# A two-layer transformer chain on one core: the recurrence's output projection, the order inside the head projections, the forget rows and the exponential's table

## The reference

```
out = (yn + bonus) * g ;  y = out @ w_out
x = layernorm(4**0.25 * x + (1 + gt1) * y)
```

```
q_a = rope(rmsnorm(q)) ; k_b = rmsnorm(kf) ; q_b = rmsnorm(qf)
logits_b = q_b k_b / 8 + cum(log f)[query] - cum(log f)[key]
```

## Time and profile before

| | |
|---|---|
| median of 3 runs | 2915.62 us (2913.86 to 2916.25) |
| the profiled execution | 2917.28 us |
| its span | 2915.5 us |
| PE busy | 2770.7 us, 95% |
| DVE, ACT, POOL busy | 1360.3, 1012.8, 300.4 us |
| mean granted clock of TensorE | 0.97 |

### The profile page before, as it was taken

The page is one execution under the profiler, slowest core; times in us unless marked ns, Lnnn a source line. Parts: engine busy times, 40 slices in busy tenths (PEclk is TensorE's granted clock), DMA queues, the critical chain, the costliest instruction groups (busy, mean ns, idle before and its releaser), DMA issues.

```text
span 2915.5 us, 46457 instructions
## 1 busy us (share of the span) xinstructions
PE 2770.7 (95%) x19096; PEld 2018.3 (69%) x19096; DVE 1360.3 (47%) x2285; ACT 1012.8 (35%) x1570; POOL 300.4 (10%) x250
## 2 busy tenths in 40 slices
PE   7999998899999899989999899999989899999999
PEld 4566666478888535678888778887565567788886
DVE  6566565243333266653333544333224776434335
ACT  5334333143422124644432333221111465323223
POOL 3232332010000003210000010000000131000000
PEclk9999999999999999999999999999979999999999
DMA  5333433222232121022232122322021001222331
GB/s 221 114 124 129 139 123 123 102 87 92 95 108 95 48 66 37 26 91 101 88 115 100 58 81 91 106 99 100 31 75 70 1 9 66 101 92 95 114 110 58
DMA packets 46292, 261.07 MB, mean 90 GB/s; under 512 B 5128, under 2 KB 7576, under 8 KB 26168
## 3 DMA queue, kind: packets, MB, share of 16 engines
q1 hardware_dynamic: 45128, 254.23, 24.8%
q10 hardware_dynamic: 1008, 4.57, 0.4%
HBM read 256.63 MB, written 2.15 MB: 89 GB/s over the span
## 4 chain that ended last, share of the span: by engine, by line
PE 87%; DVE 5%; ACT 3%; issue 1%; POOL 1%; PEld 1%; DMA 1%; SPq 0%; DVEq 0%; ACTq 0%; PEldq 0%; POOLq 0%
PE psum L214 86%; PE psum L2064 2%; PEld psum L214 1%; DMA ada_first<-in_ada_first 1%; POOL branch_in L564 0%; POOL ysum L562 0%; DVE residual L1539 0%; ACT L608 0%; POOL join L557 0%; DVE weights L248 0%; DVE residual L1531 0%; DVE keys_rstd L2675 0%; DVE cmp_blocks L2689 0%; ACT ln_in L1494 0%; ACT nsa_probs L2100 0%
## 5 line engine op out<-in xcount | busy, mean ns | idle before, releaser
L214 PE MATMUL psum<-ffn_in_hi,ffn_weights_hi 128*128 128x512 f32 x768 | 305.0, 397 | 12.4 <-DVE ffn_weights_lo L1660 7.8
L1657 ACT ACTIVATE ffn_weights_hi<-weights 128x1024 fp32r<-128x1024 f32 (+1 forms) x128 | 145.9, 1142 | 490.7 <-PE psum L214 490.7
L214 PE MATMUL psum<-ffn_in_lo,ffn_weights_hi 128*128 128x512 f32 x768 | 302.0, 393 | 0.0
L214 PE MATMUL psum<-ffn_in_hi,ffn_weights_lo 128*128 128x512 f32 x768 | 301.9, 393 | 0.0
L214 PE MATMUL psum<-ff_in_hi,ff_weights_hi 128*128 128x512 f32 x704 | 277.6, 394 | 11.5 <-DVE ff_in_lo L1545 7.2
L1657 ACT ACTIVATE ff_weights_hi<-weights 128x1024 fp32r<-128x1024 f32 (+1 forms) x120 | 137.6, 1147 | 433.4 <-PE psum L214 433.4
L214 PE MATMUL psum<-ff_in_lo,ff_weights_hi 128*128 128x512 f32 x704 | 276.7, 393 | 0.0
L214 PE MATMUL psum<-ff_in_hi,ff_weights_lo 128*128 128x512 f32 x704 | 276.3, 392 | 0.0
L1660 DVE TENSOR_TENSOR ff_weights_lo<-weights,ff_weights_hi 128x1024 fp32r<-128x1024 f32 (+1 forms) x116 | 156.3, 1347 | 253.4 <-ACT ff_weights_hi L1657 253.4
L1660 DVE TENSOR_TENSOR ffn_weights_lo<-weights,ffn_weights_hi 128x1024 fp32r<-128x1024 f32 (+1 forms) x126 | 166.9, 1327 | 110.4 <-ACT ffn_weights_hi L1657 110.3
L214 PEld LDWEIGHTS psum<-ffn_in_hi,ffn_weights_hi 128*128 128x128 f32 x768 | 146.2, 190 | 47.2 <-DVE ffn_weights_lo L1660 9.1
(11 more groups left out here) (519 smaller groups left out, 4899.3 us busy)
## 6 DMA issues: line engine op xcount, KB each, us to landing
weights<-in_ff_in SPq DMA_DIRECT2D x44, 1024.0 KB, 4.7
weights<-in_ffn_in SPq DMA_DIRECT2D x44, 1024.0 KB, 4.7
weights<-in_ada SPq DMA_DIRECT2D x80, 512.0 KB, 3.5
weights<-in_ff_out SPq DMA_DIRECT2D x16, 1408.0 KB, 5.9
weights<-in_ffn_out SPq DMA_DIRECT2D x16, 1408.0 KB, 5.9
weights<-in_rwkv SPq DMA_DIRECT2D x8, 1152.0 KB, 5.6
weights<-in_fox_qkv SPq DMA_DIRECT2D x4, 1536.0 KB, 6.4
weights<-in_rwkv SPq DMA_DIRECT2D x8, 640.0 KB, 4.0
```

The lines of the kernel that those rows point to most:

```text
L214: return nc.tensor.matmul(out, lhsT, rhs, start=start, stop=stop)
L1657: return nc.scalar.activation(sp_.hi[u][:, 0:width], slot[s][:, u * width:(u + 1) * width], ACT.Copy)
```

## The change

Four edits. The recurrence's output projection goes from `project` to `split_project`; the recurrence's output is split tile by tile on ACT (`recurred_hi`) and DVE (`recurred_lo`), PE waits for each tile of it by itself (`by_tile`), and the residual is loaded in four quarters which POOL multiplies, DVE waiting for a quarter at the head of each output tile (`x_by_tile`). In `head_inputs` the key's sum stands behind the first block of the value products and the rotation behind the second; ACT's root of the key stands ahead of its copy of the values. The clearing of the forget rows is appended to POOL's list before the head projections. And each `paired_attention` begins on ACT with an exponential of one column into an array that nobody reads.

```diff
         def residual_again(ready):
-            act_done = steps("again_act", ["scaled"])
+            done = steps("again_pool", [f"scaled{q}" for q in range(4)])
+            quarter = x_in
 
             def act(act):
-                act_done.enter(act)
                 for r in ready:
                     act.wait_ge(*reached(*r))
-                act.dma_start(x[:, :, :], d["x"][:, :, :]).then_inc(x_in[0], 16)
-                act.wait_ge(x_in[0], 32)
-                nc.scalar.activation(x[:, :, :], x[:, :, :], ACT.Copy, scale=ALPHA).then_inc(*act_done.step("scaled"))
-
-            phase(act=act)
-            return act_done, "scaled"
+                for q in range(4):
+                    act.dma_start(x[:, 2 * q:2 * q + 2, :], d["x"][:, 2 * q:2 * q + 2, :]).then_inc(quarter[q], 16)
+
+            def pool(pool):
+                done.enter(pool)
+                for q in range(4):
+                    pool.wait_ge(quarter[q], 32)
+                    nc.gpsimd.tensor_scalar(x[:, 2 * q:2 * q + 2, :], x[:, 2 * q:2 * q + 2, :], ALPHA, None, ALU.mult, ALU.bypass).then_inc(
+                        *done.step(f"scaled{q}"))
+
+            phase(act=act, pool=pool)
+            return lambda j: (done, f"scaled{j // 2}")
...
-        def split_project(halves, stream, source, ready, factor, x_ready, units_free=None, into=None, gain=None, later=None, following=None, roots=None):
+        def split_project(halves, stream, source, ready, factor, x_ready, units_free=None, into=None, gain=None, later=None, following=None, roots=None, x_by_tile=None, by_tile=False):
...
-                        if j == 0 and not roots:
+                        if j == 0 and not roots and not by_tile:
                             for r in ready[u]:
                                 pe.wait_ge(*reached(*r))
                         for k in range(half):
                             if roots:
                                 roots.between(pe, j, u, k)
-                                if j == 0:
-                                    pe.wait_ge(*reached(*ready[u][k]))
+                            if (roots or by_tile) and j == 0:
+                                pe.wait_ge(*reached(*ready[u][k]))
...
                 for j in range(KT):
                     i, s = j // 2, j % 2
+                    if x_by_tile:
+                        dve.wait_ge(*reached(*x_by_tile(j)))
...
         STEP_TILES = (2, 3, 1, 0)
 
+        unread = keep("table_unread", [P, 1])
...
             def act(act):
+                nc.scalar.activation(unread[:, :], const("rms_eps"), ACT.Exp)
                 if made is not None:
                     made.act(act, 0, TR)
...
-            pe_done = steps("heads_pe", ["nq", "fq", "nq sum", "fk", "fq sum", "v", "rot", "fk sum"])
-            act_done = steps("heads_act", ["nq sq", "fq sq", "nq std", "fk sq", "fq std", "v", "fk std"])
+            pe_done = steps("heads_pe", ["nq", "fq", "nq sum", "fk", "fq sum", "fk sum", "rot", "v"])
+            act_done = steps("heads_act", ["nq sq", "fq sq", "nq std", "fk sq", "fq std", "fk std", "v"])
...
                     for b in range(QT):
                         for k in range(KT):
                             last = mm(ps[:, V, b * P:(b + 1) * P], h[:, k, b * P:(b + 1) * P], wtile(1, 2 * KT + k), k == 0, k == KT - 1)
+                        if b == 0:
+                            pe.wait_ge(*act_done("fk sq", i))
+                            mm(ps[:, KSUM, :], blockones, sq["fk"][:, :]).then_inc(*pe_done.step("fk sum"))
+                        if b == 1:
+                            pe.wait_ge(*dve_done("nq n", i))
+                            mm(ps[:, ROT, :], cc("rot"), qn[:, :]).then_inc(*pe_done.step("rot"))
                     last.then_inc(*pe_done.step("v"))
-                    pe.wait_ge(*dve_done("nq n", i))
-                    mm(ps[:, ROT, :], cc("rot"), qn[:, :]).then_inc(*pe_done.step("rot"))
-                    pe.wait_ge(*act_done("fk sq", i))
-                    mm(ps[:, KSUM, :], blockones, sq["fk"][:, :]).then_inc(*pe_done.step("fk sum"))
...
+                    root("fk", KSUM, "fk", i)
                     act.wait_ge(*pe_done("v", i))
                     alone(act)
                     nc.scalar.activation(tile_of(out["fox_v"], i), ps[:, V, :], ACT.Copy).then_inc(*act_done.step("v"))
-                    root("fk", KSUM, "fk", i)
...
-            return out, [(dve_done, "fk", N - 1), (act_done, "fk std", N - 1)]
+            return out, [(dve_done, "fk", N - 1), (act_done, "v", N - 1)]
...
             scaled = residual_again([recurred])
-            summed = project("rwkv_out", "rwkv_out", [yout[:, k, :] for k in range(KT)], [recurred], (0, GT1), [scaled])
+
+            def recurred_hi(act, name=name, turn=turn):
+                hi_done.enter(act)
+                act.wait_ge(*reached(rec_done, name, turn - 1))
+                out_units.first(act, out_units.first_hi)
+                for k in range(KT):
+                    act.wait_ge(*reached(rec_done, name, k))
+                    nc.scalar.activation(recurred_parts[0][:, k, :], yout[:, k, :], ACT.Copy).then_inc(*hi_done.step(f"hi{k}"))
+
+            def recurred_lo(dve):
+                lo_done.enter(dve)
+                out_units.first(dve, out_units.first_lo)
+                for k in range(KT):
+                    dve.wait_ge(*hi_done(f"hi{k}"))
+                    nc.vector.tensor_tensor(recurred_parts[1][:, k, :], yout[:, k, :], recurred_parts[0][:, k, :].bitcast(F32), ALU.subtract).then_inc(
+                        *lo_done.step(f"lo{k}"))
+
+            phase(act=recurred_hi, dve=recurred_lo)
+            summed = split_project(out_units, "rwkv_out", [(recurred_parts[0][:, k, :], recurred_parts[1][:, k, :]) for k in range(KT)],
+                                   [[(lo_done, f"lo{4 * u + k}") for k in range(4)] for u in range(2)], (0, GT1), (), x_by_tile=scaled,
+                                   by_tile=True)
...
-                    heads, ready = head_inputs(parts, h, cc, ready)
+                    nsa_q = keep("heads_nsa_q", [P, 4, T], parts)
                     sides, zero_sides = forget_sides(parts, ready)
+                    phase(pool=zero_sides)
+                    heads, ready = head_inputs(parts, h, cc, ready, nsa_q)
                     with ExitStack() as own:
                         nsa_done = grouped_attention(own, heads["nsa_q"], t, cc, ready, mixed[:, 0:4, :])
-                    phase(pool=zero_sides)
```

8 lines of the change are left out of this document (6 added, 2 removed).

## The result

| | before | after |
|---|---|---|
| median of the runs (4 each) | 2915.93 us | 2898.59 us (2897.08 to 2899.59) |
| the profiled execution | 2917.28 us | 2898.09 us |
| mean granted clock | 0.97 | 0.972 |

The ratio is 0.9928, 95% interval 0.9915 to 0.9941; the same two kernels, measured twice more, gave 0.9941 (0.9927 to 0.9954) and 0.9931 (0.9918 to 0.9944). Their mean, 0.9933, is 19.4 us of 2915.62. The ratio is not the quotient of the two medians beside each other: these differ by 17.3 us here and by 15.0 and 19.3 us in the two others. The forecast was 13.6 us, 2902.0 us, with a range from 2898.0 to 2909.0. The median of 2898.59 lies just inside the range, but the ratio of 0.9928 puts the kernel at 2894.6 us and the mean of the three at 2896.2, faster than the whole range.

What follows compares the result with a forecast made beforehand. TensorE was taken to bound the kernel, holding 87% of the chain of waits. Terms 6.2 + 2.7 + 0.8 + 2.7 + 1.2 = 13.6 us gave a median of 2902.0 us, range 2898.0 to 2909.0.

Steps and rivals of the forecast that it cites:

- for clock gained elsewhere: Whole kernel: the range was said to go 3 us beyond the high end for this.
- Projection, term 6.2 us: Recurrence's output projection: split one-pass products shorten the stage from 57.6 to 51.4 us, gaining 6.2 us (2.5 to 7.3).
- the sign that the scaled quarters end before 541: Recurrence's output projection: if the forecast is right, POOL's scaled residual quarters end before 541 us.
- Order, term 2.7: End of the head projections: key sum and rotation inside the value products bring everything after 2.7 us earlier (2.4 at least).
- nothing is gained in the first turns: Head projections: in the three other turns PE never waited, so the new order gains nothing there.
- Table, term 0.8: Grouped attention's start: table load leaves the place between mask and first exponential, gaining 0.8 us (0 to 1.3).
- Rows, terms 2.7 + 1.2: Grouped attention's start: without memsets the scaling pair falls 2.7 us (or 0); clock behind it gives 1.2 (0 to 2.0).
- the stall of another cause: Attention's first scaling pair: memsets didn't make the stall, so 2.7 and 1.2 us are missing, 2905.9 us; chance 0.10.
- the clock stuck low: Recurrence's output projection: PE's clock stays low, slower, up to 2939.1 us if for all 192 products; chance 0.03.
- the late residual: Recurrence's output projection: DVE waits for the first quarter, gain 2.5 instead of 6.2 us, 2905.7 us; chance 0.12.

Runs made afterwards that it cites:

- residual_only: Kernel before with only the residual loaded in four quarters and multiplied on POOL, projection still float32; 2917.05 us, ratio 0.9992.
- sp_loads: Changed kernel with the four residual loads on SyncE's queue, behind the first two rows of weights, instead of ACT's; 2900.37 us, ratio 0.9932.
- best: sp_loads plus unread PE products in holes ahead of this projection and the head projections, and a finer order of splits; 2902.46 us, ratio 0.9936.
- proj_only: Kernel before with only the recurrence's output projection changed to the new split one; 2908.94 us, ratio 0.9962.
- loads_later: Changed kernel with the four residual loads on ACT's queue behind its source splits instead of ahead of them; 2906.02 us, ratio 0.9956.
- before_again: Kernel before, unchanged, measured again as a kernel of its own; 2919.45 us, ratio 0.9998.
- after_again: Changed kernel, unchanged, measured a second time; 2904.98 us, ratio 0.9941.
- best2: best with DVE's wait for the scaled quarter moved from ahead of the weights' split to the update of x; 2898.61 us, ratio 0.9934.
- rows_only: Kernel before with only the clearing of the forget rows moved ahead of the head projections; 2913.67 us, ratio 0.9977.
- rows_twice: Changed kernel with the six memsets made a second time at their old place behind the head projections; 2905.37 us, ratio 0.9949.
- wait_at_update: sp_loads with DVE's wait for the scaled quarter moved from ahead of the weights' split to the update of x; 2899.61 us, ratio 0.9933.

## Why the prediction was right in its mechanisms and wrong in its sum

The mechanisms held; the sum was too small. The step that failed is the clock's share in it: I counted low stretches only inside the stages whose work I changed, and put every other stage at nothing.

- What was put at 0: F and X, 1.5 us each. No work in them changed, yet the low stretch at their start is gone in all three profiles of the changed kernel. This is the largest part of what was missing.
- The margin for it was too small as well. The prediction says that the range goes 3 us beyond the high end "for clock gained elsewhere", but its end at 2898.0 lies 1.6 us beyond the 2899.6 of the high ends. With 3 us it would have been 2896.6, still a little above the mean of the three measurements, 2896.2.
- Projection, term 6.2 us. In the two profiled executions it is 57.67 to 51.5, 6.15 us, with the start at 4.69 (forecast 4.5), some nine low products (forecast 10.3) and no wait for the residual. But the profiled execution of before was one of the short ones. From POOL's end to the end of the projection the mean of six profiles with the old projection is 58.1 us and that of the five of the changed code 51.4, so the term is 6.7 us. P as a whole, 85.3 and 78.1, is 7.1 us shorter: the other 0.4 lie in the first feed-forward's first products.
- The residual: the sign that the scaled quarters end before 541 failed. They ended at 542.8, 15.9 us behind POOL's last tile where 541 meant 12.6, and it cost nothing here. A quarter took POOL 2.77 us even with DVE idle (residual_only), not 2.2.
- The conflict of POOL and DVE. The low parts of the weights took DVE 1.38 and 1.51 us in the changed kernel where they began with a multiply of POOL, and 0.69 us otherwise; in sp_loads one took 0.68 us that began 2.2 us into POOL's second multiply. The Trainium skill (GPSIMD Engine Reference, 1. Specifications) says that GpSimd shares its SBUF interfaces with VectorE and contends with instructions that have two SBUF inputs, as these have: the slow ones agree, the one in the middle of a multiply shows no contention. It cost nothing in the changed kernel. In best some 2.0 of the 2.77 us of PE's hole are this slowing (an estimate: 3.95 us for POOL's first quarter against 2.77, and 1.52 for the split against 0.69); the rest is the place of the wait.
- Order, term 2.7: 2.5 alone. In the three profiles of the changed kernel H is 3.6 us shorter; most of the other 1.1 lies at its first 16 products, which took 15.2 to 15.6 us instead of 16.4. proj_only, which has the old order, is 0.7 us shorter there too, and loads_later, which has all four edits, is not (16.3). I had said that nothing is gained in the first turns.
- Table, term 0.8: 0.9, and up to 1.8 while the memsets are still there. Rows, terms 2.7 + 1.2: 2.7 and 1.7, the latter with the doubt above. Together A fell from 96.3 to 91.0, 5.3 us against 4.7. The two overlap: alone they gave 2.1 and 4.4.

By the table the changed stages sum to 7.1 + 3.6 + 5.3 + 1.5 + 1.5 = 19.0 us, against 19.4 by the mean of the ratios. That they agree so well is in part luck, for the stages outside the table move by several us from profile to profile: the profiles of before and after differ by 19.2 us in all, those of before_again and after_again by 13.7.

Open is why the low stretches in F, in the first products of H and in X come and go. In F, 5 of 6 profiles with the same code as before up to there have it and none of the eight with the new projection and a cold start, but residual_only lacks it too, and best and best2 have it. F's length goes with how late the clock rose a few microseconds earlier; which edit, if any, decides that was only argued. The rivals: the stall of another cause is refuted by rows_only and rows_twice; the clock stuck low did not occur; the late residual is real but had 0.2 us or less of effect until PE ran its first tile at the full clock.

## What to carry to other kernels

A hole in TensorE's stream can be paid for twice, once as idle time and once as a low clock behind it. Stages that nobody touched can lose or gain such a low stretch: widen the range on the gaining side by one (1.5 us here) for each later stage that begins with one in the profile before, and on the other side for each that could get one. When a single stage gets shorter and the kernel doesn't, look for these stretches first, and profile the unchanged kernel more than once before you call a difference of this size an effect. Put a wait right ahead of the instruction that needs it: a wait for the residual ahead of the next weights' split cost nothing until the stage got faster, and then was part of a hole of 2.8 us. And read which event an engine's first instruction really waited for, since a wait ahead of it in the queue can hide an earlier start of 1.6 us.

## What the runs showed of the hardware

- A memset of 1 x 2048 or 128 x 2048 on POOL takes 1.8 to 1.9 us. Beside memsets a pair of DVE scalings of 128 x 384 with two column operands ended 0.2 us behind the end of one: 0.87 us alone, 2.65 to 3.58 beside them. A scaling of 128 x 8 took 1.86 us through one memset and 3.60 through two (before_again), against 0.23 alone. DVE's reductions (0.42 us), masks (0.55 us) and a product of two arrays of 128 x 256 (0.42 us) in the same stretch were not slowed.
- A low part of 128 x 512 on DVE (a subtraction of two arrays) that began within 0.2 us behind the start of a POOL multiply of 128 x 1024 took 1.38 to 1.56 us (after, sp_loads, best, loads_later); one that began 1.2 us or more into it took 0.68 to 0.69 (sp_loads, best2, wait_at_update). POOL's multiply took 2.77 us with DVE idle (residual_only), and the first of the four 3.15 to 4.53 beside DVE's series of low parts.
- Four float32 products (eight records) that nobody reads, in the hole ahead of the projection in best2, brought the clock up: it was 0.50 in the 2.8 us ahead of them, 0.77 while they ran, and 1.00 for the 45 us of products behind them. Without them some nine products ran at 0.50. In best the clock was at 1.00 for the first tile and fell behind the next hole of 2.77 us. These and the first real one in PE's timeline:

```profile
523.83 4.75 PE L214 MATMUL psum<-branch_in,const_all 128*128 128x512 f32 x8
528.47 0.47 PE L214 MATMUL psum<-recurred_hi,rwkv_out_weights_hi 128*128 128x512 f32 x1
```

- Products of 512 columns from split parts start 0.227 us apart at the full clock: ten steps in 2.27 us between these two rows of the kernel after. At the level 0.50 they started 0.427 us apart. The Trainium skill gives 215.7 ns for back-to-back products of 512 columns at 2.4 GHz (TensorE: Matmul & The Clock Gate, "Wait — 56ns, not 53.3ns?"); the rows here stay 5% above it.

```profile
549.67 0.39 PE L214 MATMUL psum<-recurred_lo,rwkv_out_weights_hi 128*128 128x512 f32 x1
...
551.94 0.39 PE L214 MATMUL psum<-recurred_hi,rwkv_out_weights_lo 128*128 128x512 f32 x1
```
